# A gated recurrence of eight heads: projection steps ahead of products on TensorE, weight pieces ahead of exponentials on ScalarE

## The reference, cut to what matters

```python
def _chunk_gla(q, k, v, g, s0):      # per chunk of 64 tokens
    G = jnp.cumsum(gc, axis=2)
    decay = jnp.exp(jnp.where(tri, G[:, :, :, None, :] - G[:, :, None, :, :], -jnp.inf))
    scores = jnp.einsum('bhik,bhjk,bhijk->bhij', qc, kc, decay)
    o = jnp.einsum('bhij,bhjv->bhiv', scores, vc) + jnp.einsum('bhik,bhkv->bhiv', qc * jnp.exp(G), s)
...
def _odd_mixer(h_ctx, h_lat, w_in, lower_bounds, layer, out_norm, ctx_out):
    fq, f_fwd, f_bwd, fi, fog = _split(h @ w_in, ODD_SIZES)
    q = _heads(jax.nn.silu(fq), HGRN_HEADS)
    ...
    for d, f in enumerate((f_fwd, f_bwd)):
        log_f = jnp.logaddexp(jnp.log(lb[d]), jnp.log1p(-lb[d]) + jax.nn.log_sigmoid(_heads(f, HGRN_HEADS).astype(jnp.float32)))
        k = -jnp.expm1(log_f)
        dirs.append(_directional_scan(q, k, i, log_f, n_ctx, reverse=(d == 1)))
    o_lat = _gated_readout(dirs[0][1] + dirs[1][1], og[:, :, n_ctx:], out_norm)
```

## Time and profile before

| what | us |
|---|---|
| median of three runs | 2694.2 |
| profiled execution, device time | 2697.0 |
| its span | 2695.2 |
| TensorE busy | 2390.4 (89%) |
| VectorE busy | 1466.9 (54%) |
| ScalarE busy | 1030.6 (38%) |
| GpSimd busy | 201.8 (7%) |

### The profile page before, as it was taken

How to read it: one execution, slowest core, us unless ns; L and a number is a source line. 1 busy time by engine, 2 the same in 40 slices (tenths; PEclk the granted TensorE clock), 3 DMA queues, 4 the chain that set the end, 5 groups by cost and what they waited for, 6 DMA issues and landing times.

```text
span 2695.2 us, 35087 instructions
## 1 busy us (share of the span) xinstructions
PE 2390.4 (89%) x14650; PEld 1861.3 (69%) x14650; DVE 1466.9 (54%) x2319; ACT 1030.6 (38%) x1736; POOL 201.8 (7%) x294
## 2 busy tenths in 40 slices
PE   5987788999997888877998998979999998979899
PEld 3834455888884766667997753347877787867899
DVE  5416745556555476765455306555566544871544
ACT  3233434222224344444444325544332324321553
POOL 0001200000000022220000002100200200000110
PEclk8998989999998999988998999989999999989899
DMA  6235641534421444333643214432443433253443
GB/s 264 73 125 205 244 162 49 172 133 146 149 95 69 141 156 156 96 123 101 203 172 139 88 51 136 154 140 83 147 148 139 148 125 134 103 192 107 151 168 136
DMA packets 172478, 372.25 MB, mean 138 GB/s; under 512 B 7040, under 2 KB 99456, under 8 KB 158112
## 3 DMA queue, kind: packets, MB, share of 16 engines
q1 hardware_dynamic: 172320, 370.01, 39.0%
HBM read 339.55 MB, written 30.44 MB: 137 GB/s over the span
## 4 chain that ended last, share of the span: by engine, by line
PE 73%; DVE 12%; ACT 8%; issue 3%; DMA 2%; POOL 1%; SPq 0%; DVEq 0%; ACTq 0%; POOLq 0%
PE ps L169 73%; DVE sb_R L200 4%; ACT sb_R L248 2%; DVE sb_R L232 1%; DVE sb_WP L200 1%; DMA sb_R<-mod_w 1%; DVE sb_H L200 1%; PE ps L179 1%; DMA sb_slot<-mod_w 1%; DVE sb_X L217 1%; ACT L244 1%; ACT sb_R L254 1%; ACT sb_WP L254 1%; DVE sb_cst L200 1%; DVE sb_R L229 1%
## 5 line engine op out<-in xcount | busy, mean ns | idle before, releaser
L169 PE MATMUL ps<-sb_HP,sb_WP 128*128 128x512 f32 (+1 forms) x5568 | 1051.9, 351 | 65.0 <-DVE sb_WP L200 39.7
L169 PEld LDWEIGHTS ps<-sb_HP,sb_WP 128*128 128x128 f32 x5568 | 899.7, 194 | 195.6 <-issue 39.8
L200 DVE TENSOR_TENSOR sb_WP<-sb_slot,sb_WP 128x1024 fp32r<-128x1024 f32 x356 | 438.3, 1237 | 639.5 <-ACT sb_WP L254 639.4
L254 ACT ACTIVATE sb_WP<-sb_slot 128x1024 fp32r<-128x1024 f32 x356 | 373.9, 1057 | 784.9 <-PE ps L169 772.7
L169 PE MATMUL ps<-sb_XP,sb_WP 128*128 128x512 f32 (+1 forms) x2592 | 450.9, 336 | 10.2 <-DVE sb_XP L200 10.2
L169 PEld LDWEIGHTS ps<-sb_XP,sb_WP 128*128 128x128 f32 x2592 | 398.6, 190 | 62.6 <-DVE sb_XP L200 12.2
L200 POOL TENSOR_TENSOR sb_R<-sb_R 128x128 f32<-128x128 f32 (+2 forms) x194 | 147.2, 784 | 1857.7 <-ACT sb_R L248 1423.7
L169 PE MATMUL ps<-sb_R 128*32 128x64 f32 (+8 forms) x2088 | 176.7, 290 | 81.7 <-DVE sb_R L200 29.8
L169 PEld LDWEIGHTS ps<-sb_R 128*32 128x32 f32 (+5 forms) x2088 | 125.5, 154 | 147.5 <-issue 74.7
L200 DVE TENSOR_TENSOR sb_R<-sb_R 128x256 f32<-128x256 f32 (+3 forms) x398 | 198.0, 533 | 30.4 <-ACT sb_R L248 27.4
L248 ACT ACTIVATE sb_R<-ps 128x512 f32<-128x512 f32 (+1 forms) x208 | 99.4, 514 | 128.4 <-PE ps L169 124.9
(11 more groups left out here) (137 smaller groups left out, 1977.1 us busy)
## 6 DMA issues: line engine op xcount, KB each, us to landing
sb_slot<-mlp_w SPq DMA_DIRECT2D x32, 2048.0 KB, 9.1
sb_slot<-mod_w SPq DMA_DIRECT2D x22, 2048.0 KB, 8.1
sb_R<-ada_w SPq DMA_DIRECT2D x12, 2048.0 KB, 7.4
sb_slot<-ada_w SPq DMA_DIRECT2D x24, 1024.0 KB, 4.8
sb_slot<-ffn_w_gate SPq DMA_DIRECT2D x22, 1024.0 KB, 5.3
sb_slot<-ffn_w_up SPq DMA_DIRECT2D x22, 1024.0 KB, 7.8
sb_slot<-ffn_w_down SPq DMA_DIRECT2D x10, 2048.0 KB, 7.8
sb_slot<-odd_w_in SPq DMA_DIRECT2D x32, 512.0 KB, 7.2
```

Source lines behind the costliest of these rows:

```text
L169: return self.e.matmul(out, w, x, start=start, stop=stop, skip_group_check=True)
L200: return BLANK if self.e is None else self.e.tensor_tensor(out, a, b, op)
L254: return self.e.activation(out, a, ACT.Copy) if scale is None else self.e.activation(out, a, ACT.Copy, scale=scale)
```

## The change

Two orders within a round are turned, and nothing else.

On TensorE, the projection of the next head is given to `together` as the first generator rather than the third: step k now stands ahead of the diagonal products (round 0) or ahead of product k - 1, and ahead of the read-out's sum. The modulation products stay last.

On ScalarE, the copies of weight pieces are taken out of `project_act` into a generator of their own, `pieces_act`, that stands first: the copy of rounds 1, 3, 5 and 7 comes ahead of that round's exponential. The sigmoids and the logarithm stay where they were. VectorE's, GpSimd's and SyncE's queues are the same.

```diff
-    def project_act(self, act, ahead, h):
-        e, S = act.on("odd.proj"), self.sets[h % 2]
+    def pieces_act(self, ahead):
         for k in range(KT):
             if k % 2 == 1:
                 next(ahead)
+            yield
+
+    def project_act(self, act, h):
+        e, S = act.on("odd.proj"), self.sets[h % 2]
+        for k in range(KT):
             yield
         if h:
             e.wait_ge("og", h - 1)
...
         for h in range(8):
-            together(self.mix_pe(pe, h), self.read_pe(pe, h - 1), *([self.project_pe(pe, h + 1)] if h < 7 else []), steps(more, 11))
+            together(*([self.project_pe(pe, h + 1)] if h < 7 else []), self.mix_pe(pe, h), self.read_pe(pe, h - 1), steps(more, 11))
...
-        together(self.project_act(act, ahead, 0))
+        together(self.pieces_act(ahead), self.project_act(act, 0))
         for h in range(8):
-            together(self.mix_act(act, h), self.cross_act(act, h), self.read_act(act, h - 1),
-                     *([self.project_act(act, ahead, h + 1)] if h < 7 else []), steps(more, 11))
+            together(*([self.pieces_act(ahead)] if h < 7 else []), self.mix_act(act, h), self.cross_act(act, h), self.read_act(act, h - 1),
+                     *([self.project_act(act, h + 1)] if h < 7 else []), steps(more, 11))
```

## The result

The changed kernel took 2677.1 us in the median of four runs beside 2695.5 us for the kernel before; the ratio is 0.9928, 95% interval 0.9910 to 0.9946. The time is inside the predicted range of 2661 to 2679, 10 us above the predicted 2667, and outside the forecast's own 2662 to 2672. Its profiled execution had a span of 2670.0 us against 2695.2.

What follows compares the result with a forecast made beforehand. No engine is full; each head is a chain across engines, lengthened by weight-copy waits and TensorE work ahead of the last projection step. Per-head gains of 26.6 us, less 0.7, plus 1.4, give 27.3: 2667 us, range 2661 to 2679.

Steps and rivals of the forecast that it cites:

- The chain through the head: In each head no engine is full; weight-copy waits and TensorE work ahead of the last projection step needlessly lengthen the path.
- the first rival: Step 0 at low clock outlasts VectorE's running sums, or keys block the subtraction: gain 8 to 21 us, about 2678; chance 0.18.
- Step 7's place (B): On TensorE, the next head's last projection step directly follows the previous step and one product: 2.55 us earlier.
- (b): TensorE work after the last projection step must keep up; head 1's cross scores start at 992.97, not 996.94: 4.0 us.
- Part 2: TensorE's projection of the next head ahead of products; bounded between 9 and 20 us over seven heads.
- head 6: TensorE alone bounds this head; it loses a low-clock step 0 and product 6, VectorE 0.3 behind: 4.2 us gained.
- the diagonal's wait: VectorE's diagonal waited 0.70 us for low-clock TensorE in three heads; filling the gap ahead of two gives 1.4 us.
- The filler (c): Step 0 of the projection after next fills TensorE's 2.75 us wait for VectorE's running sums, fitting by 0.4 us, costing nothing.
- The copies (A): ScalarE's weight copies ahead of exponentials remove VectorE waits, 0.96 us in round 5 and 0.76 in round 3: 1.72 us.
- the trace leans against it: Judged that VectorE's subtraction and GpSimd's keys don't exclude each other for whole instructions, from a subtraction taking 1.48, not 1.23 us.
- the 21 to 27: Total gain in us if VectorE's two-input SBUF instructions and GpSimd's SBUF reads exclude each other for a whole instruction.
- subtraction first: If round 5's subtraction precedes GpSimd's keys, the keys end at 987.99, still ahead of product 5 at 988.14.

Runs made afterwards that it cites:

- the cut keys: The changed kernel with GpSimd multiplying only 8 of 256 columns of the keys of halving 5: 2675.1 us, ratio 0.9923, stage 240.0 us.
- the kernel with both tables ahead: The changed kernel with ScalarE's two table loads ahead of their waits, the study's fastest: 2672.7 us, ratio 0.9908; again 2671.0 us, 0.9905.

## Why the prediction was right, and where its size was off

**The chain through the head** was read rightly: no engine full, two things on the path that need not be there. Removing both shortened every one of the seven heads. The time alone says less than it seems: the four runs give a gain of 18.4 us, below the forecast's own 22 to 32, and 2677 is the number of the first rival (8 to 21, about 2678), which the range was widened to take in. Its mechanism, the filler past F at the low clock in six heads, isn't what the trace shows. It is the stage, 22.6 us by itself, that bears the forecast out, at its lower edge.

**Step 7's place (B).** 2.55 us was forecast for step 7's start, and measured from product 5 it is 2.54. Up to the cross scores (b) left 2.25 of it (3.97 less 1.72), and head 1 gained 2.10: from product 6 to the modulation products it takes 0.54 in place of 0.37. Part 2 as a whole had 19.7 in the sum (27.3 less 7.6 for the copies, below) and measured 17.2. The step at fault is head 6: 4.2, and 0.7 more for the diagonal's wait, were forecast, 3.0 measured. I let TensorE save its whole low-clock step there, with VectorE 0.3 behind. TensorE then waited for VectorE ahead of products 2 and 4, 1.8 us in all, where before it had no break:

```profile
1145.62 0.69 PE L169 MATMUL ps<-sb_R 128*128 128x128 f32 x4 [1.17 <-DVE sb_R L200]
...
1151.59 0.68 PE L169 MATMUL ps<-sb_R 128*128 128x128 f32 x4 [0.64 <-DVE sb_R L200]
```

VectorE in its turn waited 1.89 us for GpSimd's product on `sb_cst` there (at 1142.33), a wait that the slower TensorE had hidden. Next to it, head 0's diagonal found TensorE at the low clock and VectorE waited 1.21 us (0.51 more than the 0.70 before), and head 5's, behind the modulation products, 0.90: forecast 0.45 and 0.7. At heads 4 and 6 the waits of 0.70 went, as forecast.

**The filler (c)** costs nothing at the seams in heads 1, 2, 3, 4 and 6, as forecast: F comes 0.65 us behind it, at the full clock. The first rival, step 0 past F at the low clock (4.18 us), happened only in front of head 0; in front of head 5 it ran past F at the full clock (2.37), which the sum had. The rule of the Trainium skill, "TensorE: Matmul & The Clock Gate", section "Part 1: The HAM clock gate", that activity releases the full clock, holds in these rows: the granted clock over the stage went from 0.95 to 0.98, and with step 0 behind the diagonal again it was 0.95.

**The copies (A)** failed in size, and this is the larger of the two steps at fault: "the trace leans against it". In the per-head sum the copies stand with 1.72 in heads 1, 3 and 4, 0.76 in heads 2 and 5 and 0.96 in head 0, 7.6 us in all. Against TensorE's order alone the stage gained just that, 247.6 to 240.0, in the kernel without the keys of halving 5; with them it gained 5.3. The missing 2.3 us are the meeting of GpSimd and VectorE. The Trainium skill, "SBUF — State Buffer", section "Who interferes with whom", had said it: a VectorE instruction with two SBUF inputs contends with a GpSimd instruction that reads SBUF, and the lock is exclusive. The rows of the two engines agree with that, and the 22.6 us lie in the 21 to 27 that the prediction gave for it. I had weighed it by one row of a subtraction stretched by 0.25 us, which was misread: it had begun 0.40 us before GpSimd was done. The difference at 980.17 of the changed kernel began 0.46 before the first keys instruction was done and was stretched by 0.33. The wait comes out 0.14 shorter than the overlap in both, so the old row fits the same exclusion, and didn't lean against it. And I had found the case "subtraction first" free, because the keys would still end ahead of product 5. They did, at 981.30 against 982.06. What I left out is what VectorE does next: its differences met the keys that had been pushed back. And the trace of before had the case in full: in heads 6 and 7 no subtraction stands there, and the same group took 1.74 and 1.72 us. In the second trace of that kernel it was 1.09 in head 6, and the keys were held instead. The row of head 6:

```profile
1175.62 1.74 DVE L200 TENSOR_TENSOR sb_R<-sb_R 128x256 f32<-128x256 f32 x3
```

So of the 4.7 us between 27.3 and 22.6, 2.3 are the meeting (shown by the cut keys) and 1.9 are head 6 (4.9 forecast, with the 1.4 for the diagonal's waits put on heads 4 and 6, where they were). 0.45 is head 4, which I didn't separate further. The other five heads are within 0.1 of their terms, once the meeting is taken off.

**The time, 10 us above the forecast.** Five are the stage, and one is the median of the kernel before, which was 2695.5 beside the changed kernel, in place of 2694.2. Three comparisons gave ratios of 0.9928, 0.9923 and 0.9928, that is 19 to 21 us, while the stage says 22.6, or 0.9916, which lies inside all three intervals. What may lie between: stretches at the low clock outside the stage. The first long run of projections behind it took 24.61 us before and 25.83 after, the same 192 matmuls behind the same wait:

```profile
1228.62 24.61 PE L169 MATMUL ps<-sb_HP,sb_WP 128*128 128x256 f32 x192 [5.92 <-DVE sb_HP L200]
```

```profile
1201.27 25.83 PE L169 MATMUL ps<-sb_HP,sb_WP 128*128 128x256 f32 x192 [5.92 <-DVE sb_HP L200]
```

This row isn't chance: it took 24.6 in both traces of the kernel before and 25.8 in all three of the changed one. From head 7's sums to the end the traces of the kernel before took 1503.9 and 1504.0 us, the three of the changed kernel 1505.3, 1507.1 and 1503.7, and the seven other traces of the study, each of a kernel that differs from the one before in this stage alone, 1506.2 to 1508.3. So some of the gain seems to be given back behind the stage, 1.4 us on average for the changed kernel; what sets it, and the rest of the 4 us, stays open.

## What to carry to other kernels

Where an in-order engine has a short urgent instruction and a longer one with slack, look whether the longer one fits into the idle time ahead of the urgent one's wait: there it cost nothing here, and behind it its own consumer waits. The last step of a producer whose result opens the next iteration belongs directly behind its input, ahead of work that the next engine wants later. And when an instruction is moved in time, ask not only whom it meets but what is queued behind both partners; a meeting that the new order will create may stand in the old trace already, as here, in an iteration that lacks the moved instruction.

## What the runs showed of the hardware

GpSimd can be held for most of a VectorE instruction with two inputs in SBUF: 8 columns of multiplication took 1.46 us beside a subtraction of 1.22, and 0.66 without it (256 columns take 1.00). It works the other way too: two differences and a multiplication of VectorE that take 1.09 us took 1.74 beside keys. Which engine loses can change from one execution to the next: in head 4 of the kernel with both tables ahead the keys were held for 2.45 us and the group took 1.09 in one trace, 1.44 and 1.75 in the other. TensorE's clock depends on what came before, but not on the last gap alone: behind a 2.75 us gap the diagonal of head 1 took 1.81 and the two steps after it 5.46 us with step 0 put back, and 1.16 at the full clock in the kernel before, as did that of head 2 in the earlier trace rows. With the gap filled it took 1.16 in heads 1, 2, 3, 4 and 6 alike, and a step 2.34. And the stage, taken between two fixed instructions, repeated within 0.1 us over two traces of the kernel before and three of the changed one, and within 0.5 over two of the best, for the reason just given; the point where it begins moved by up to 7 us.
